# Ordering the projections K, Q, V and rotating before the head norm factors, in a two-layer encoder trunk

## The reference

```
q, k, v = split(h @ w_qkv, [1024, 1152])       # 16 query heads, 2 key heads, 2 value heads, head size 64
q = rope(rms_norm(q, q_gain), positions)       # the norm is over the 64 channels of a head
k = rope(rms_norm(k, k_gain), positions)
rope(x) = [x1*cos - x2*sin, x2*cos + x1*sin]   # x1, x2 are the halves of a head
scores, softmax with a sink per head, then @ v, then @ w_o
```

## Time and profile before

| what | value |
|---|---|
| median of 3 runs | 2443.24 us |
| the profiled execution | 2443.44 us |
| its span | 2441.6 us |
| PE busy | 2324.0 us, 95% |
| DVE busy | 1222.6 us, 50% |
| POOL busy | 770.9 us, 32% |
| ACT busy | 670.3 us, 27% |
| first scores of the attention start at | 233.86 us |
| first unit of the WO projection starts at | 331.68 us |

### The profile page before, as it was taken

The page is one execution under the profiler, slowest core; times in us unless marked ns, Lnnn a source line. Parts: engine busy times, 40 slices in busy tenths (PEclk is TensorE's granted clock), DMA queues, the critical chain, the costliest instruction groups (busy, mean ns, idle before and its releaser), DMA issues.

```text
span 2441.6 us, 28960 instructions
## 1 busy us (share of the span) xinstructions
PE 2324.0 (95%) x10184; PEld 1860.5 (76%) x10184; DVE 1222.6 (50%) x1518; ACT 670.3 (27%) x904; POOL 770.9 (32%) x569
## 2 busy tenths in 40 slices
PE   2897999899999999998999999999899999999999
PEld 1776668688888888886788788888678888888887
DVE  7764756756656665435333541343655444455311
ACT  3322632323322322222322220121333223223210
POOL 1111321255345445221212112111143554455211
PEclk9996999999999999998999999999999999999999
DMA  6243141221221222311343321121011111111112
GB/s 253 90 134 97 48 166 39 74 70 61 78 86 52 85 86 71 101 43 35 129 129 129 109 82 57 61 73 47 26 44 52 61 43 44 59 52 43 52 52 86
DMA packets 76754, 189.22 MB, mean 77 GB/s; under 512 B 23441, under 2 KB 25361, under 8 KB 76177
## 3 DMA queue, kind: packets, MB, share of 16 engines
q1 hardware_dynamic: 58288, 127.64, 16.1%
q10 hardware_dynamic: 18400, 60.69, 7.0%
HBM read 170.48 MB, written 16.78 MB: 77 GB/s over the span
## 4 chain that ended last, share of the span: by engine, by line
PE 47%; issue 47%; POOL 6%; POOLq 0%; DVE 0%; ACT 0%; DVEq 0%
PE pp L1398 28%; PE pp L1653 19%; POOL w_lo L378 5%; POOL pr L391 1%; POOL w_lo L417 0%; PE pp L1475 0%; POOLq L437 0%; POOLq L377 0%; DVE x L1192 0%; ACT w_hi L687 0%; POOLq L390 0%; POOLq L395 0%; POOLq L385 0%; POOLq L433 0%; POOLq L421 0%
## 5 line engine op out<-in xcount | busy, mean ns | idle before, releaser
L378 POOL TENSOR_TENSOR w_lo<-w_raw,w_hi 128x1024 fp32r<-128x1024 f32 x146 | 359.5, 2463 | 1352.6 <-ACT w_hi L452 1352.6
L1398 PE MATMUL pp<-h_hi,w_hi 128*128 128x512 f32 x1824 | 601.9, 406 | 38.0 <-DVE h_lo L976 23.0
L1398 PE MATMUL pp<-h_lo,w_hi 128*128 128x512 f32 x1824 | 592.4, 400 | 0.0
L1398 PE MATMUL pp<-h_hi,w_lo 128*128 128x512 f32 x1824 | 591.2, 400 | 0.0
L1398 PEld LDWEIGHTS pp<-h_hi,w_hi 128*128 128x128 f32 x1824 | 344.7, 191 | 129.9 <-issue 21.8
L1398 PEld LDWEIGHTS pp<-h_hi,w_lo 128*128 128x128 f32 x1824 | 348.1, 191 | 85.2
L1398 PEld LDWEIGHTS pp<-h_lo,w_hi 128*128 128x128 f32 x1824 | 348.6, 191 | 83.5
L1262 DVE SCALAR_TENSOR_TENSOR x<-pp,mod,x 128x512 f32<-128x512 f32 x336 | 252.2, 751 | 242.1 <-PE pp L1653 242.1
L452 ACT ACTIVATE w_hi<-w_raw 128x1024 fp32r<-128x1024 f32 x146 | 154.2, 1057 | 706.3 <-PE pp L1398 562.7
L1653 PE MATMUL pp<-c_hi,w_hi 128*128 128x512 f32 x672 | 265.6, 395 | 0.0
L1653 PE MATMUL pp<-c_lo,w_hi 128*128 128x512 f32 x672 | 265.6, 395 | 0.0
(11 more groups left out here) (159 smaller groups left out, 2278.8 us busy)
## 6 DMA issues: line engine op xcount, KB each, us to landing
w_raw<-weights SPq DMA_DIRECT2D x194, 512.0 KB, 3.5
mod_t<-mod_w ACTq DMA_DIRECT2D x64, 512.0 KB, 4.0
mod_first<-mod_w SPq DMA_DIRECT2D x16, 512.0 KB, 15.4
mod_late<-mod_w ACTq DMA_DIRECT2D x2, 4096.0 KB, 19.1
v_dram<-v_out ACTq DMA_DIRECT2D x16, 512.0 KB, 5.4
vf<-v_dram ACTq DMA_DIRECT2D x16, 512.0 KB, 3.3
x<-x_in SPq DMA_DIRECT2D x4, 1024.0 KB, 8.9
qf<-q_dram SPq DMA_DIRECT2D x32, 128.0 KB, 2.5
```

Of the source, the lines that this page charges most:

```text
L378: nc.gpsimd.tensor_tensor(out=w_lo[:, s, :, :], in0=w_raw[:, s, :, :], in1=w_hi[:, s, :, :].bitcast(f32), op=ALU.subtract).then_inc(lo_don ...
L1398: last = T.matmul((pp[s] if tile is None else tile)[:, cs], w[:, s, k, :], r[:, k, cs], start=(k == 0 and w is w_hi and r is hi), stop=(k ...
```

## The change

- The order of the units is keys, queries, values: U_K = 0, U_Q = 1 to 8, U_V = 9. The keys are in slot 0 of pair 0. A query's half a is now in slot 1 and its half b in slot 0 of the next pair. The order of the weights in memory stays, so SP's loads take other indices.
- Keys: ACT squares directly from PSUM and copies with the gain as its scale. The swap transfers start from that copy, before the norm. DVE rotates first, and multiplies the factors in last. The four kf transfers are issued in the middle of query pair 0's work on ACT.
- Queries: DVE does the six instructions of rotation with cos and sin themselves, ahead of the factors, and then two multiplies by the factors in pp[2], in place of the two of cos and sin. The reciprocal stands between the rotation's first three and last three instructions.
- The hooks: head_squares of a query is in slot 1's unit after k = 4, head_spread in the following slot 0's unit after k = 2; the last spread stands behind the V unit. mod_columns(2) and (3) become hooks after k = 2 in units (2,1) and (4,1).
- ACT copies and squares the halves a in first_half(j), which also holds the split of the next slot 1 weights, behind the load_mod of that turn.
- The mod steps stand in pairs: two ahead of the key rotation, two behind it, and for each j < 3 two after the rotation and two after the factors. The number of mod steps and of loads is as before.
- q_out is four semaphores, one for each query pair, in place of one. save_q waits for the two last multiplies.
- The values' transposes go through the two halves of pp[1] by turns.
- SP: the w_raw load of pair 5 stays ahead of the attention's q loads; that of pair 6 moves behind them (before, it stood ahead).

The core of the diff:

```diff
-U_Q, U_K, U_V = 0, KC, KC + 1
+U_K, U_Q, U_V = 0, 1, KC + 1
...
+            def first_half(j):
+                act.wait_ge(gemm, U_Q + 2 * j + 1)
+                if j >= 2:
+                    act.wait_ge(q_turned, j - 1)
+                nc.scalar.activation(qa[:, 1 - j % 2, :], pp[1][:, :], ACT.Copy).then_inc(evac[1], 1)
+                split_hi(j + 1, 1)
+                act.wait_ge(evac[1], j + 1)
+                nc.scalar.activation(tmp[:, 0, :], qa[:, 1 - j % 2, :], ACT.Square).then_inc(q_sq, 1)
...
             act.wait_ge(gemm, U_K + 1)
+            nc.scalar.activation(tmp[:, 0, :], pp[0][:, :], ACT.Square).then_inc(q_sq, 1)
+            nc.scalar.activation(qa[:, 0, :], pp[0][:, :], ACT.Copy, scale=kgain).then_inc(evac[0], 1)
+            split_hi(1, 0)
...
+            head_roots(0, KV)
+            load_mod(2, 0)
+            load_mod(3, 1)
+            first_half(0)
+            for j in range(4):
+                slot = 1 - j % 2
+                act.wait_ge(gemm, U_Q + 2 * j + 2)
+                nc.scalar.activation(qb[:, slot, :], pp[0][:, :], ACT.Copy).then_inc(evac[0], 1)
+                act.wait_ge(q_bc, j + 1)
+                act.wait_ge(evac[0], j + 2)
+                nc.scalar.activation(tmp[:, 1, :], qb[:, slot, :], ACT.Square).then_inc(q_sq, 1)
+                split_hi(j + 2, 0)
...
+                if j < 3:
+                    load_mod(4 * j + 4, 0)
+                    load_mod(4 * j + 5, 1)
+                head_roots(j + 1, 4)
+                if j < 3:
+                    load_mod(4 * j + 6, 0)
+                    load_mod(4 * j + 7, 1)
+                    first_half(j + 1)
...
+                dve.wait_ge(q_sq, 2 * j + 3)
+                V.tensor_tensor(out=tmp[:, 0, :], in0=tmp[:, 0, :], in1=tmp[:, 1, :], op=ALU.add).then_inc(q_sum, 1)
...
+                turn(c, a, qgain_a, cos[:, :])
+                turn(d, b, qgain_b, sin[:, :])
+                own(V.tensor_tensor(out=c, in0=c, in1=d, op=ALU.subtract))
+                head_reciprocals(j + 1, 4)
+                turn(d, b, qgain_b, cos[:, :])
+                turn(a, a, qgain_a, sin[:, :])
+                V.tensor_tensor(out=d, in0=d, in1=a, op=ALU.add).then_inc(q_turned, 1)
...
+                if j < 3:
+                    mods(2)
+                dve.wait_ge(q_turned, j + 1)
+                dve.wait_ge(q_bc, j + 2)
+                V.tensor_tensor(out=c, in0=c, in1=pp[2][:, :], op=ALU.mult).then_inc(q_cs, 1)
+                V.tensor_tensor(out=d, in0=d, in1=pp[2][:, :], op=ALU.mult).then_inc(q_cs, 1)
+                if j < 3:
+                    mods(2)
...
             normed_pair(0)
+            unit(1, 0, h_hi, h_lo, hooks={3: lambda: head_squares(0)})
+            unit(1, 1, h_hi, h_lo, hooks={1: lambda: head_spread(0), 4: lambda: head_squares(1)})
             for j in range(3):
+                unit(2 + j, 0, h_hi, h_lo, hooks={2: lambda: head_spread(j + 1)})
+                hooks = {4: lambda: head_squares(j + 2)}
...
+                unit(2 + j, 1, h_hi, h_lo, hooks=hooks)
+            head_spread(4)
```

More of the change, by code:

```diff
@@ L323, in save_q @@
             def save_q(j):
[L325 removed]
+                sp.wait_ge(q_cs, 2 * j + 2)
                 for i in range(4):
@@ L329, in save_q @@
                         sp.dma_start(q_dram[:, j // 2, 32 * part:32 * part + 32, head, :].rearrange("n d t -> d n t"),
-                                     src[32 * i:32 * i + 32, j % 2, :].rearrange("d (n t) -> d n t", t=CHUNK)).then_inc(q_out, 16)
-            with sp.Fori(1, 3) as pair:
+                                     src[32 * i:32 * i + 32, 1 - j % 2, :].rearrange("d (n t) -> d n t", t=CHUNK)).then_inc(q_out[j], 16)
+            with sp.Fori(1, 4) as pair:
                 for s in range(2):
[L334 to L339, removed]
+                    load_block(pair, s, -1)
+            save_q(0)
+            load_block(4, 0, -1)
+            load_block(4, 1)
+            save_q(1)
+            for s in range(2):
+                load_block(5, s)
+            save_q(2)
             save_q(3)
-            load_block(6, 1)
             def load_q(t, n, g):
@@ L354, in _ @@
                     load_q(n * 2 + g, n, g)
-            with sp.Fori(7, U_MLP[0] // 2 + 1) as pair:
+            with sp.Fori(6, U_MLP[0] // 2 + 1) as pair:
                 for s in range(2):
@@ L594, in _ @@
                 nc.scalar.activation(v_s[:, 4 * j:4 * j + 4, :],
-                                     pp[3][:, 0:HALF].rearrange("p (n c) -> p n c", n=4), ACT.Copy).then_inc(v_cp, 1)
-            act.wait_ge(k_roped, 2)
-            for g in range(KV):
-                for part in range(2):
-                    act.dma_start(kf[32 * part:32 * part + 32, g, PAD:],
-                                  oa[64 * part + 32 * g:64 * part + 32 * g + 32, 0, :]).then_inc(kf_in, 16)
+                                     pp[1][:, columns_of(j % 2)].rearrange("p (n c) -> p n c", n=4), ACT.Copy).then_inc(v_cp, 1)
             def exps(t, b):
@@ L1114, in _ @@
-            for r, op in ((slice(0, 64), ALU.subtract), (slice(64, 128), ALU.add)):
-                V.tensor_tensor(out=oa[r, 0, :], in0=tmp[r, 0, :], in1=tmp[r, 1, :], op=op).then_inc(k_roped, 1)
+            head_reciprocals(0, KV)
+            mods(2)
+            dve.wait_ge(trig, 2)
+            dve.wait_ge(k_swap, 32)
+            own(V.tensor_tensor(out=oa[:, 0, :], in0=qa[:, 0, :], in1=cos[:, :], op=ALU.mult))
+            own(V.tensor_tensor(out=qb[:, 0, :], in0=qb[:, 0, :], in1=sin[:, :], op=ALU.mult))
@@ L1167, in _ @@
             dve.wait_ge(sinks_in, 2)
-            dve.wait_ge(q_out, 16 * 8 * 4)
+            for j in range(4):
+                dve.wait_ge(q_out[j], 16 * 8)
             dve.wait_ge(kf_in, 16 * 4)
```

150 lines of the change are left out of this document (53 added, 97 removed).

## The result

The changed kernel took 2420.31 us (median of 4 runs, 2419.71 to 2425.68) against 2443.15 for the kernel before (4 runs, 2442.19 to 2444.69): a ratio of 0.9913, with a 95% interval of 0.9900 to 0.9926. It is faster by 22.8 us by the medians, 18 to 24 by the interval. The forecast was 2424, its range 2416 to 2437; the direction and the range held. The profiled execution is the longest of the four: 2425.68 us, span 2423.9, mean granted clock 0.979, where the other three lie within 0.7 us of each other at 0.985 to 0.986. Two far slower executions are left out of all medians: one of the changed kernel in e1 (2558.87 us, granted clock 0.857) and one of the kernel before beside e1 to e4 (8297.88 us).

The account below looks back on a forecast made before the run. TensorE bound the kernel, 95% busy, losing time before the first scores to stalls, low clock and tail. Scores moving from 233.86 to 214.8 gave 2443.4 - 19.1 = 2424.3, say 2424; own range 2419 to 2429, 8 in 10 within 2416 to 2437.

Parts of the forecast that it names:

- (a): Unit (1,0): ACT's square and copy now precede the high split, so TensorE begins 1.1 us later; K's squares don't stall.
- (b): Unit (1,1): TensorE waits 3.8 us for w_lo, then 3.1 at the squares hook, both with low clock; ends at 122.7.
- the collision: GpSimd's low split of (2,0) meets DVE's back-to-back run before the sum: DVE loses 2.0 to 2.3 us.
- The price of a fall: Clock falling after a stall: slow squares and five slow pairs cost 1.1 + 2.1 = 3.2 us, as much as the stall.
- (c): Steady query pairs: sum ready at T + 3.5, hook at T + 7.0, so no stall; next weight chain just hidden.
- T: End of a unit (., 0), the second half of a Q; forecast at 134.7, 160.7 and 185.9.
- (d): Tail from V unit's end at 199.9: multiplies done 203.35, save and reload 11.5 with hand-overs, scores at 214.8.
- R1: Start better than (b): no clock fall in one or both stalls, or no collision; 2416 to 2421; chance 0.14.
- R2: Squares alone bring the clock down, 3.2 x 4 for K, Q1, Q2, Q3; 2437; chance 0.10.
- R3: Weight chain of (c) late by 2 to 3 us in three pairs, clock behind it; 2439; chance 0.10.
- R4: Slower: same place, late-issued mod loads landing late; landings of 16 give 2448; chance 0.05.
- R5: Queries' stalls go but come back as key waits of the same size; 2443; chance 0.03.

Follow-up runs that it names:

- e1: The changed kernel once more, unaltered: median 2421.22 us, ratio 0.9920 against the kernel before.
- e4: Changed kernel with the high split of unit (2,0) moved on ACT behind the kf issues and two mod loads: 2418.28 us, ratio 0.9900.
- e3: Changed kernel with ACT's copy and high split of Q0's first half ahead of the sines and K's roots: 2416.21 us, ratio 0.9896.
- e2: Changed kernel with two DVE mod steps moved ahead of the wait for K's spread: 2416.91 us, ratio 0.9894.
- e7: Changed kernel with the six rotation instructions put back behind the wait for the spread in all four query pairs: 2448.93 us, ratio 1.0019.
- e8: Kernel before with only its hooks later, squares after k=5, spread after k=1 of the pair's second unit: 2438.89 us, ratio 0.9979.
- e10: Changed kernel with hooks earlier, squares of Q1 to Q3 after k=2, mod_columns after k=1: 2425.03 us, ratio 0.9919.
- e9: Changed kernel with the six rotation instructions behind the wait for the spread in the last query pair only: 2431.20 us, ratio 0.9948.
- e5: Changed kernel with the repairs of e2 and e3, and the first two mod steps also ahead of K's reciprocal: 2412.29 us, ratio 0.9868.
- e6: e5 with the last query pair's eight stores split over SP's and ScalarE's queues, four each: 2408.87 us, ratio 0.9859.

## Why the prediction was right

**(a) Unit (1,0), +1.1 forecast, +0.2 measured.** ScalarE's order is as forecast; the high split at 78.22 is 1.6 later than the one at 76.66 in the earlier trace rows (1.9 forecast). What I had too long is above all the low split, 3.3 from the earlier trace rows. It took 2.74, and DVE paid: 2.77 at 79.87, for a TENSOR_SCALAR whose like (L1066, at 83.94) takes 0.69. In these rows whichever engine comes second waits, so the mis-sized term was the duration of a split, taken from a place with another neighbour.

**(b) The bad spot.** The wait for w_lo was forecast at 3.8 and measured 3.31, the sum of squares at 113.2 and measured 111.17 + 1.21 = 112.4, the hook's wait 3.1 and 2.86, the collision 2.0 to 2.3 and 1.9, unit (1,1)'s end 122.7 and 122.8. All three mechanisms were shown singly: e3 took the first wait, e2 the second, e4 the collision. That the unit's end came out to 0.1 is partly luck, since sizes erred and cancelled: unit (1,0) and the waits were shorter than forecast, but the squares behind the second took 3.58 in this execution, where 3.1 stood, and seven pairs were slow instead of five; in e1 the squares took 1.95, and the scores came at 211.3. The price of a fall, 3.2, was read off one stall. The prediction says that after each stall the squares take 3.05; its own have 1.95 at 155.22, and the kernel before has 3.07, 3.49 and 3.57 at its other three.

**(c) The steady pairs.** T was forecast at 134.7, 160.7 and 185.9; it was 134.9, 160.8 and 185.9. The sum of squares was ready 3.6 after T, the bound of 0 for squares without a stall was the right one, and the collision (138.43 in DVE's rows, and again at 164.38 and 189.45) was absorbed. The low split for (3,1) ended at 159.9, 0.9 us before TensorE wanted it, with 0.7 forecast. One mod load came 0.93 us late behind that chain (DVE at 158.57), and DVE still stood idle for 2.26 before the next sum. The working for this step was sound, but I had not seen how much hung on the early rotation: e7's expectation, mine, put it at 7 us, all in the tail. It also keeps the mod steps ahead of mod_columns, and that is what e7 and e8 show the price of. Nor does the working see what held the sum back in the kernel before, the mod steps ahead of it (e10).

**(d) The tail.** V unit's end 199.9 and 199.75, multiplies done 203.35 and 203.2, scores 214.8 and 214.3. The eighth issue started 4.6 after the first (5.3 forecast), landing 3.1 (3.4), load 2.7 (2.6), together 10.4; hand-overs took the other 0.7 of 11.1, with 0.2 forecast. The lower bound of this step, 10.9, is a wrong sum: 5.3 + 3.4 + 2.6 are 11.3, and the measured 11.1 lies below that. DVE's MEMSET at 211.45 marks the end of the last store.

**The sum.** 19.1 us forecast for the first scores, 19.5 measured in the profiled execution, 22.5 in e1's. The median gained 22.8. The missing 3 to 4 us are the clock: against e1's, the profiled execution lost 3.0 before the scores, in the fall behind step (b)'s second wait, and 1.8 in attention. The other three executions near 2420 were not traced; that they are like e1's is argued from their time and mean clock (0.985 to 0.986). The prediction allowed 2 or 3 either way for phases of the clock and took its marks from one execution.

**The rivals.** The median of 2420.3 lies in the forecast's own 2419 to 2429 and in R1's 2416 to 2421, so the time does not decide between them; the traces do. R1, no clock fall in one of the stalls or no collision: fell; both stalls came with a fall in all the traces that keep them (the kernel after, e1, e7, e9, e10), and the collision was there. What varied is the fall's length, by some 3 us. R2, squares alone bring the clock down: fell, no squares without idle ahead of them are followed by a slow row in any trace here. R3 and R4, a late weight or mod load: fell, with 0.9 us to spare. R5, keys as the new wait: fell, kf was issued at 106.76. What stays open: what of the gain the new order of the units, the place of the mod steps and the four separate store semaphores bring. None of them was tried alone.

## What to carry to other kernels

Split work at the input that comes late: multiply the late factor in last, and look at who else is queued behind that wait on its engine, since there, as e7 shows, most of the price may lie. Carry marks unit by unit and subtract at each hook what is ready from when it is wanted; the two places where that came out negative were the two stalls, and moving a few lines at each gave some 12 us more (e5). Look also at what stands ahead of an urgent instruction in its engine's queue, as the mod steps stood ahead of the sum. Moving a hook later is the weaker remedy: it hides a late input until the input's own successors are late (e8).

## What the runs showed of the hardware

The same program with the same waits gave two traced executions 4.5 us apart, by what the clock did. Behind 3.29 us of idle in the middle of matmuls the granted clock stayed high in e1 (443.65) and in the kernel before (465.86) and fell to the low level for 3.4 us in the kernel after (449.43); behind the 3.3 us ahead of unit (1,1) it fell in all seven traces that have that wait. Idle of 0.93 followed by 1.95 us of squares brought a slow stretch of 3.3 us in e4; 1.23 and 1.95 brought none in e8 (at 91.70), 1.47 with the squares did (118.49). Squares without idle never did. So a stall's price here is itself plus 0 to 4.5 us (the squares 1.7 and seven pairs 2.8 longer, at 112.44), and the totals of one profile against one other tell nothing of a change below 5 us.

Eight 128 KB stores over two queues instead of one brought the start of the last issue from 4.6 to 1.85 us behind the first (e5, e6), but they were slower to land, 3.3 to 4.4 us against 3.1: half of the gain was lost.
